# Attention's probabilities are scaled by a diagonal matmul while they are turned

## The reference

```python
logits = jnp.einsum('bqhd,bqkhd->bqhk', q, kg) * HEAD_DIM ** -0.5
logits = jnp.where(valid[:, :, None, :], logits, -jnp.inf)
p = jax.nn.softmax(logits, axis=-1)
return jnp.einsum('bqhk,bqkhd->bqhd', p, vg)
```

## Time and profile before

| | us |
|---|---|
| median of 3 runs | 3033.44 (3024.99 to 3033.66) |
| the profiled execution | 3033.91 |
| its span | 3032.1 |

### The profile page before, as it was taken

How to read it: one execution, slowest core, us unless ns; L and a number is a source line. 1 busy time by engine, 2 the same in 40 slices (tenths; PEclk the granted TensorE clock), 3 DMA queues, 4 the chain that set the end, 5 groups by cost and what they waited for, 6 DMA issues and landing times.

```text
span 3032.1 us, 38694 instructions
## 1 busy us (share of the span) xinstructions
PE 2741.1 (90%) x16047; PEld 2489.3 (82%) x16047; DVE 1318.2 (43%) x2743; ACT 664.7 (22%) x1182; POOL 818.6 (27%) x521
## 2 busy tenths in 40 slices
PE   6999999999989999957689945859999999999998
PEld 4999999999868999944443534639989999999998
DVE  4122222222628999968842255134561222222225
ACT  5111111110333332213333431041131111111113
POOL 5422232232321111232500025003443223323220
PEclk8999999999979999976679656579999999999999
DMA  3211111110112322232223021025211111111101
GB/s 126 70 42 42 43 57 55 42 56 25 63 28 63 98 79 96 84 133 83 93 76 137 1 41 16 0 82 182 85 35 56 43 42 53 59 43 52 46 15 57
DMA packets 182811, 189.72 MB, mean 63 GB/s; under 512 B 18524, under 2 KB 164176, under 8 KB 179784
## 3 DMA queue, kind: packets, MB, share of 16 engines
q1 hardware_dynamic: 162568, 133.17, 14.6%
q0 software_dynamic: 2944, 35.65, 3.2%
q10 hardware_dynamic: 17136, 18.53, 1.8%
HBM read 160.10 MB, written 25.78 MB: 61 GB/s over the span
## 4 chain that ended last, share of the span: by engine, by line
PE 68%; DVE 18%; issue 7%; ACT 2%; DMA 2%; POOL 1%; SPq 1%; DVEq 0%; ACTq 0%; POOLq 0%
PE ps L240 33%; PE ps L249 16%; PE ps L1835 3%; PE ps L1818 2%; PE ps L1216 2%; PE ps L820 2%; DVE x_T L752 2%; DVE k_index_T_high L1133 1%; PE ps L842 1%; DVE new_small L1131 1%; PE ps L1527 1%; PE ps L98 1%; PE ps L653 1%; DVE probs L866 1%; PE ps L603 1%
## 5 line engine op out<-in xcount | busy, mean ns | idle before, releaser
L240 PE MATMUL ps<-normed_split,f_weights_split 128*128 128x344 f32 x6336 | 1001.8, 320 | 0.0
L240 PEld LDWEIGHTS ps<-normed_split,f_weights_split 128*128 128x128 f32 x6336 | 998.6, 188 | 0.7 <-issue 0.2
L249 PE MATMUL ps<-f_hidden_split,f_down_split 128*128 128x344 f32 x2880 | 456.6, 319 | 0.0
L249 PEld LDWEIGHTS ps<-f_hidden_split,f_down_split 128*128 128x128 f32 x2880 | 453.9, 188 | 0.0
L293 DVE TENSOR_TENSOR f_hidden<-f_silu,ps 128x344 f32<-128x344 f32 x132 | 67.7, 513 | 858.9 <-PE ps L240 850.5
L603 PE MATMUL ps<-normed_split,in_weights_split 128*128 128x344 f32 (+1 forms) x2520 | 403.6, 321 | 7.3 <-POOL normed_split L129 6.1
L603 PEld LDWEIGHTS ps<-normed_split,in_weights_split 128*128 128x128 f32 (+1 forms) x2520 | 396.3, 187 | 11.2 <-POOL normed_split L129 6.5
L303 DVE SCALAR_TENSOR_TENSOR x_T<-ps,x_T 128x344 f32<-128x344 f32 x480 | 248.0, 517 | 196.9 <-PE ps L249 196.9
L209 POOL TENSOR_TENSOR f_hidden_split<-f_hidden,f_hidden_split 128x344 fp32r<-128x344 f32 x132 | 122.7, 930 | 569.4 <-DVE f_hidden_split L296 569.4
L201 POOL TENSOR_TENSOR f_weights_split<-f_weights_raw,f_weights_split 128x1024 fp32r<-128x1024 f32 x88 | 210.8, 2419 | 0.0
L177 ACT ACTIVATE f_silu<-ps 128x344 f32<-128x344 f32 x132 | 59.9, 455 | 650.4 <-PE ps L240 650.4
(11 more groups left out here) (299 smaller groups left out, 2803.9 us busy)
## 6 DMA issues: line engine op xcount, KB each, us to landing
f_weights_raw<-in_w_gate SPq DMA_DIRECT2D x44, 512.0 KB, 3.9
f_weights_raw<-in_w_up SPq DMA_DIRECT2D x44, 512.0 KB, 4.0
f_down_raw<-in_w_down SPq DMA_DIRECT2D x44, 512.0 KB, 3.7
in_weights_raw<-in_w_in SPq DMA_DIRECT2D x34, 512.0 KB, 3.8
gates_T<-projected ACTq DMA_DIRECT2D x16, 516.0 KB, 2.6
gates<-gates_T SPq DMA_DIRECT2D x16, 516.0 KB, 4.4
x_meanwhile<-x_T SPq DMA_DIRECT2D x1, 4128.0 KB, 12.0
x_T<-x_meanwhile SPq DMA_DIRECT2D x1, 4128.0 KB, 17.2
```

The source lines that it names most:

```text
L240: mm = nc.tensor.matmul(m.ps[:, NCH * half + c, :CH], m.wh[:, 2 * e + half, a, k * P:(k + 1) * P], m.xn[:, k, b, cols(c)], start=(k == 0 a ...
L249: mm = nc.tensor.matmul(m.ps[:, bank, :CH], w[:, e, a, o * P:(o + 1) * P], m.hh[:, (2 * p + e) % 4, b, cols(c)], start=(e == 0 and t == 0) ...
```

## The change

The normalising pass of ScalarE goes. VectorE, when it has inverted the sums, multiplies the 128x128 identity by them, one value per partition, which gives a diagonal matrix in one of two buffers. The turn is no longer a transpose but a matmul with the probabilities as weights and this diagonal as the moving operand: its output is the turned block with each query's column already scaled. The semaphore `scaled`, for which the turn waits, is now raised by the diagonal. `keep_turned`, `pv` and all else stay.

```diff
@@ mix_memory
     m.st = sb("softmax_stats", [P, 2, 4])
+    m.diag = place(nc, w + 14080)("inverse_diagonals", [P, 2, P])
@@ att_pe, turn(n)
         for k in range(b + 1):
-            mm = nc.tensor.transpose(m.ps[:, 4 + k // 4, (k % 4) * P:(k % 4 + 1) * P],
-                                     m.prob[:, n % 2, k * P:(k + 1) * P], m.ident[:])
+            mm = nc.tensor.matmul(m.ps[:, 4 + k // 4, (k % 4) * P:(k % 4 + 1) * P],
+                                  m.prob[:, n % 2, k * P:(k + 1) * P], m.diag[:, n % 2, :], start=True, stop=True)
         mm.then_inc(s.turned, 1)
@@ att_dve, invert(n)
         nc.vector.reciprocal(m.st[:, n % 2, 3:4], m.st[:, n % 2, 2:3]).then_inc(s.inv, 1)
+        dve.wait_ge(s.inv, n + 1)
+        nc.vector.tensor_scalar(m.diag[:, n % 2, :], m.ident[:], m.st[:, n % 2, 3:4], None, ALU.mult).then_inc(s.scaled, 1)
@@ att_act
-    def normalise(n):
-        b, h = STEPS[n]
-        w = (b + 1) * P
-        act.wait_ge(s.inv, n + 1)
-        nc.scalar.activation(m.prob[:, n % 2, :w], m.prob[:, n % 2, :w], ACT.Identity,
-                             scale=m.st[:, n % 2, 3:4]).then_inc(s.scaled, 1)
@@ att_act, the loop over n
         samples(n)
-        if 1 <= n <= n_last:
-            normalise(n - 1)
         if n < n_last:
             exp(n)
```

## The result

| | before | after |
|---|---|---|
| median, us | 3033.66 (3024.99 to 3037.34, 7 runs) | 3053.05 (3044.59 to 3056.68, 7 runs) |
| profiled execution / span | 3033.91 / 3032.1 | 3053.05 / 3051.1 |

What follows compares the result with a forecast made beforehand. VectorE was taken to pace attention's first stretch and TensorE to fill the fourth at 1.2 GHz, ScalarE bounding none. Terms 4.6 + 4.0 + 3.0 + 4.1 + 12.1 = 27.8 us on 3033.9 gave 3062 us, range 3040 to 3080.

Steps and rivals of the forecast that it cites:

- ScalarE's pass is worth nearly nothing: Attention, 64 activations, 49.4 us in total: removing them gains 0.7 us, once, after the key dots of step 20.
- The diagonal on VectorE, +4.6: First stretch of attention: a 222 ns product delays the bias pass by 0.24 us in 19 steps, +4.6 us.
- Bounds 0.10 [...] to 0.40: First stretch: limits on the diagonal's added time per step in us, giving 2 to 8 us in all.
- Hidden: Third and fourth stretches: VectorE idle four fifths and two thirds of the time, so its diagonal adds nothing.
- TensorE's second pass: Turn as fp32 matmul: one more instruction a block, +0.213 us at 1.2 GHz, +0.107 at 2.4.
- the third stretch +4.1: Third stretch, 132 us: first turns of step pairs are on the path, 36 blocks longer, +4.1 us, bounds 3.8 to 8.
- the second 3.0: Second stretch, 41 us, b = 5: longer turns add 0.7, 1.0 and 1.3, together +3.0 us, bounds 0 and 6.
- the 4.0: First stretch: TensorE backlog from longer turns, 1 us for each of four blocks of steps, +4.0 us, bounds 0 and 14.
- The fourth stretch, +12.1: Last 71 us of attention, TensorE back to back at 1.2 GHz: 45 blocks in 23 groups cost +12.1 us.
- rival A: Fourth stretch: clock rises to 2.4 GHz, b = 2 step falls from 3.88 to 2.6 us; total 3035; chance 0.11.
- B: Rival: weight loads bind at 0.31 us an instruction; fourth stretch +21, third +10, total 3078 us; chance 0.07.

Runs made afterwards that it cites:

- the summing form: Against the kernel after the change: VectorE makes the diagonal by the same instruction's form that also writes out a sum; 3037.45 us, ratio 1.0012 to the kernel before.
- the unread diagonal: Against the kernel before: VectorE additionally makes the diagonal, which nobody reads; normalising pass and transposes stay; 3059.62 us, ratio 1.0075.
- no scaling: Against the kernel before: normalising pass left out with nothing in its place, the turn waits for the reciprocal alone; 3028.39 us, ratio 0.9977.

## Why the prediction was right in sum and wrong in its parts

*ScalarE's pass is worth nearly nothing*: right. Forecast 0.7, in the profile without it 1 to 2 us.

*The diagonal on VectorE, +4.6*: right for the 0.286 us instruction (forecast 0.222), +4.5 with the summing form. It failed as the whole cost, and it failed in "Bounds 0.10 [...] to 0.40": I took the duration from two rows that show no wait for GpSimd. The one of 512 columns (L1148, at 1549.62) ran beside none of its instructions. Of the 64 of one column (L871), seven did run inside one, and took 153 to 154 ns all the same, so this row gave no warning. Three diagonals of 5.5 to 5.8 us on the path are 16 us more; from the change to the summing form stretch 1 fell by 16.9. "Hidden" in the fourth stretch held only as long as TensorE was slow: at the raised clock the diagonal costs 0.24 us a step in b = 1. The trace of before held the warning about GpSimd elsewhere, unread by me. A tensor-by-scalar of four columns took 3.90 us and ended when GpSimd's instruction beside it did; the last two lines show one of one column that wasn't held:

```profile
1343.26 8.84 POOL L1032 TENSOR_TENSOR x_T<-x_T,samples_attention 128x4096 f32<-128x4096 f32 x1 [21.61 <-DMA samples_attention<-q_sample_rows]
...
1347.24 5.14 DVE L1108 TENSOR_TENSOR new_small<-new_index_rows 8x256 f32<-8x256 f32 x1
1352.42 0.41 DVE L1110 TENSOR_REDUCE new_small<-new_small 8x4 f32<-8x256 f32 x1
1352.86 3.90 DVE L1111 TENSOR_SCALAR new_small<-new_small 8x4 f32<-8x4 f32 x1
1356.79 0.15 DVE L1112 TENSOR_TENSOR new_small<-new_small 8x4 f32<-8x4 f32 x1
...
1391.41 8.86 POOL L1032 TENSOR_TENSOR x_T<-x_T,samples_attention 128x4096 f32<-128x4096 f32 x1
1396.07 0.15 DVE L871 TENSOR_SCALAR softmax_stats<-softmax_stats 128x1 f32<-128x1 f32 x1
```

L1108 runs to 1352.38, some 0.3 us beyond the end of GpSimd's multiplication at 1352.10. L1111 ends at 1356.75, and the next of GpSimd's instructions at 1356.73. The Trainium skill has this as a rule ("SBUF — State Buffer", Who interferes with whom): VectorE's plain tensor_scalar, but not the form that writes out its accumulator, can take a port pair that it shares with GpSimd, and whoever comes second waits for the whole instruction of the other. The trace and the experiment with the summing form agree: 5.46 us against 0.35. It was a rule that spoke against this change, and I had weighed another.

*TensorE's second pass*: the size a block and a group was right (4.63 us a step at 1.2 GHz, 4.63 measured). In the third stretch +4.1 was forecast and 2.6 measured; in the second 3.0 and 1.2 to 2.0. In the first the 4.0 failed: measured 0.0 to 0.2, with the diagonal elsewhere or absent. The mean clock over 1338 to 1528 us was 0.74 with the diagonal on ScalarE, against 0.66 before; that this paid for the longer turns is likely, but no run isolates it.

*The fourth stretch, +12.1*: failed. From the samples' last values to the last reciprocal the change brought -8.6 (4a and 4b), because rival A came true, at a chance of 0.11: the clock rose, to a step of 2.5 us where A had 2.6. The reason given against it, that the density hardly changes, did not keep the clock down. The rule of the Trainium skill that stood for A ("TensorE: Matmul & The Clock Gate", PE-mode transpose), that transposes don't count as activity, was not the ground either, since the transposes turned twice raised the clock as well (0.50 to 1.00); my reading of the earlier trace rows holds. A small slip besides: B's own terms, 8.9 and 5.9 us above the forecast's, give 3077 and not 3078.

So 8.6 became 21.4 in the first stretch and 12.1 became -8.6 in the last, and two errors of 13 and -21, with some smaller ones, left a forecast of 27.8 beside 19.4. That the total fell into the range is luck: the errors happened to cancel. Without the experiments the number would have passed for an understanding.

What stays open: why 0.83 us of turn in 3.88 us leaves the clock at 1.2 GHz for the whole stretch and 1.48 to 1.58 in 4.5 to 4.6 lifts it. The runs show that it does, in both kinds of turn, and no more.

## What to carry to other kernels

Before an instruction is put on VectorE, look at what GpSimd runs at that time, and price it from rows of about its size that stand beside such an instruction: the row of one column ran unhindered where those of 4 and 128 columns waited; another form of the instruction, or ScalarE, may be free of the wait, as both were here. A stretch in which TensorE is back to back and still at 1.2 GHz need not be at its limit: here an added pass cost less than nothing. So price such a stretch at both clocks, give both a fair chance, and ask which chain sets the pace once TensorE is fast. And cut the comparison by stretches even where the total fits.

## What the runs showed of the hardware beyond that

Transposes of data that had just been transposed made a kernel faster by 0.32%: 45 blocks more of 128 columns, in a stretch that went from 61.1 to 46.4 us. In all eight kernels with a longer turn in the last 24 steps the clock came up there between 0.6 us before and 7 us after the start of step 42's bias pass, stayed up for 34 to 38 us and was at 0.50 again for the last 6 to 14 us; in the three with the turn unchanged (before, the unread diagonal, no scaling) it stayed at 0.50 to the end.

Ahead of attention the same instructions took 1331.6 us in the profile of one version and 1339.4 to 1344.2 in the others. Scatter of this size is why parts are compared by stretches here, and only the medians between kernels.
